# First compression layer on two halves of TensorE's output partitions in turn, and the spatial bias as one rounded product over two parts, in a two-block transformer kernel

## The chip, the cores and the metric

The kernel runs on one core of one Trainium2 chip. The metric is the device time of one execution in microseconds (us); lower is better. The time before is the median of three executions, 1076.14 us (1074.05 to 1076.87).

## What is computed

Two transformer blocks run one after the other on 256 tokens of width 1024, all in float32. Two small places of them matter here. In the first block, keys and values are compressed: blocks of 32 tokens, 16 apart, are flattened and go through two layers.

```python
def compress_blocks(src, pos, w1, w2):
    ...
    blk = src[:, idx] + pos[None, None, :, None, :]
    blk = blk.transpose(0, 1, 3, 2, 4).reshape(B, nc, NSA_KV_HEADS, CMP_BLOCK * HEAD_DIM)
    return jax.nn.silu(blk @ w1) @ w2
...
k_cmp = rms_norm(compress_blocks(kc..., cmp_pos, cmp_k_w1, cmp_k_w2), k_norm_g[0])
v_cmp = compress_blocks(vc..., cmp_pos, cmp_v_w1, cmp_v_w2)
```

In the second block, one of three branches is a spatial gate: a causal 128 by 128 mix per group of 64 features, plus a bias per group and position.

```python
def spatial_gating(u, v, ln_g, ln_b, w_s, b_s):
    v = layernorm(v, ln_g, ln_b).reshape(B, nc, CHUNK, SG_GROUPS, SG_GROUP_DIM)
    w = jnp.where(causal[None], w_s, jnp.zeros_like(w_s))
    mixed = jnp.einsum('gts,bcsgd->bctgd', w, v) + b_s.T[None, None, :, :, None]
    return u * mixed.reshape(B, S, SG_WIDTH)
```

## The kernel before

All weights come as one stream of 128x128 blocks, eight to a slot of 512 KB, in the order of their use. SyncE's queue loads slots into a ring of six (`ring`, slot_full per place); a slot is loaded again when TensorE has given it back (`give_back`, semaphore slot_used). Most products are computed to nearly float32 precision out of rounded (fp32r) parts: ScalarE rounds a slot (`round_slot`, L1321), VectorE subtracts to get the low part (`split_slot`, L1760), and TensorE's `project` adds three rounded products for each block (high by high, high by low, low by high). At most four slots are rounded ahead (`HALVES`). Two slots are taken as they come, unrounded: the first-layer weights of the compressed keys (`cmp_k_w1`) and of the values (`cmp_v_w1`). Here they are called slot A and slot B; the next ones, A+2, A+3, A+4, belong to the projections `ma0`, `ma1`, `ma2`.

ScalarE and VectorE each run one written-out program. Before an operation that reads the PSUM tile of some name, the helpers `output` and `taken` first call `ahead(name)`, which rounds (or splits) all slots up to three past the one from which that name's last product read (`slot_at[name]`). So the slot that a tile is booked on sets which roundings stand ahead of its reader in ScalarE's queue.

PSUM has eight banks; `plan_psum` gives the names of a list their banks in turn, and `claim` makes TensorE wait until the bank's previous user has been read. In the list around the change, banks 0, 1 and 2 go round: `qa0` 2, `qa1` 0, `qa2` 1, `qa3` 2, `cmp_hid_k` 0, `cmp_hid_v` 1, `ma0` 2.

The first place (L874 to L888): after `project("qa3")` and the sum of squares of `qa2`, TensorE makes `cmp_hid_k`: 16 products in plain float32, 35 rows of windows of the tokens as stationary part, 64 columns of weights moving, into partitions 0 to 34 of bank 0. Then come the sum of squares of `qa3` (`sum_squares`, a 128x128 by 128x256 float32 product that waits for ScalarE's square of `qa3`, L1337), then 16 products for `cmp_hid_v` in bank 1. A float32 product is two weight loads and two matmuls ("passes") in the trace. Then come `sb_scores(0)` and `project("ma0")`. ScalarE copies `cmp_hid_k` (L1383), makes the inverse norm of `qa3` (`inv_rms`, L1345 and L1349), and copies `cmp_hid_v`. VectorE multiplies `qa3` by it (`normalise`, L1789), which frees bank 2.

The second place (`spatial`, L1149): eight times, spread between the attention heads of the second block, a float32 product of the gate is followed by a second one that adds the bias: a 128x128 matrix of ones by `lines`, 128x256 of which only partition 0 is not zero. GpSimd has loaded `lines` (L1296 to L1301) near 309 us, in the first MLP, whose loops on ScalarE and VectorE are `for m in range(KF)` (L1567, L1544; L2095, L2108, L2023).

Of the kernel before, what the change touches and what calls it, by code (L numbers as in the profile page):

```python
# [28 lines left out]
P = 128  # L29
# [12 lines left out]
CMP_STRIDE = 16  # L42
SLOT = 8
RAW_GATES = 4
MIX_BANKS = (3, 3, 4, 4, 5, 6)
# [51 lines left out]
def stream_chunks():  # L97
# [26 lines left out]
    for name in ("cmp_k_w1", "cmp_v_w1"):  # L124
        for j in range(CMP_CHUNKS):
            out.append((name, j, None))
# [207 lines left out]
def build(nc, stream, ada, c_d, x_t, mem_t, cols_d, mats_d, buckets_d, table_d, pos_d, cmp_w2_d,  # L334
# [4 lines left out]
    with ExitStack() as ctx:  # L339
        def sb(name, shape, dt=F32):  # L340
            return ctx.enter_context(nc.sbuf_tensor(name, shape, dt))

        def sem(name):
            return ctx.enter_context(nc.semaphore(name))
# [31 lines left out]
        ada_ring = sb("ada_ring", [P, ADA_RING, D])  # L376
# [3 lines left out]
        ident_rounded = sb("ident_rounded", [P, P], F32R)  # L380
        cols = sb("cols", [P, N_COLS])
# [40 lines left out]
        lines = sb("lines", [P, 1024])  # L422
        buckets, bias_line, sg_b = lines[0:33, 0:512], lines[0:8, 512:1024], lines[0:1, :]
# [28 lines left out]
        sg_ln = ada_ring[:, 2, :].rearrange("p (w f) -> p w f", w=2)  # L452

# [48 lines left out]
        sg_ready = sem("sg_ready")  # L502
        branches_added = sem("branches_added")
# [151 lines left out]
        def _(pe):  # L655
# [218 lines left out]
            for w, n in enumerate("kv"):  # L874
                evacuated(pe, n + "c")
                if n == "v":
                    sum_squares("qa3", "halves")
                name = f"cmp_hid_{n}"
                ps = claim(name)
                for i in range(CMP_CHUNKS):  # L880
                    chunk = at["chunk"]
                    pair = take_plain()
                    for j in (2 * i, 2 * i + 1):
                        ins = mm(ps[0:CMP_ROWS, 0:HD], kc_windows[:, w, 2 * j:2 * j + 545:CMP_STRIDE],
                                 pair[:, j % 2 * HD:(j % 2 + 1) * HD], j == 0, j == 2 * CMP_CHUNKS - 1)
                    if i < CMP_CHUNKS - 1:
                        give_back(ins, chunk)
                done(ins, name)  # L888
# [260 lines left out]
            def spatial(b, c):  # L1149
                name = f"sg{b}{c}"  # L1150
                ps = claim(name)
                mm(ps[:, 0:T], sg_v[:, c, b * P:(b + 1) * P], sg_w[:, 2 * b:2 * b + 2, :], True)
                done(mm(ps[:, 0:T], mat("ones"), lines[:, b * T:(b + 1) * T], stop=True), name)

            for i in range(12):
# [23 lines left out]
                if i == 2:  # L1179
                    pe.wait_ge(sg_ln_ready, TT)  # L1180
                    pe.wait_ge(sg_w_ready, 1)
                for n in SPATIAL_AT.get(i, ()):
                    spatial(*divmod(n, TT))
# [39 lines left out]
        def _(pool):  # L1223
# [74 lines left out]
            pool.dma_start(sg_b, sg_b_d).then_inc(loaded["sg"], 16)  # L1298
            pool.wait_ge(loaded["sg"], 48)
# [11 lines left out]
        def _(act):  # L1311
# [138 lines left out]
            for w, n in enumerate("kv"):  # L1450
                copy(cmp_sb[:, w, :].rearrange("p (r c) -> p r c", r=2), f"cmp_hid_{n}",
                     bank(f"cmp_hid_{n}")[0:CMP_ROWS, 0:HD].unsqueeze(1).to_broadcast([CMP_ROWS, 2, HD]))
                if n == "k":
                    inv_rms("qa3", HD, lambda: taken("qa1"))
# [114 lines left out]
            for m in range(KF):  # L1569
# [7 lines left out]
                if m:  # L1577
                    act.wait_ge(hidden_raw, m)
                    round_hidden(m - 1)
            act.wait_ge(hidden_raw, KF)  # L1580
# [168 lines left out]
        def _(dve):  # L1749
# [349 lines left out]
            for m in range(KF):  # L2099
# [10 lines left out]
                if m:  # L2110
                    rest_of_hidden(m - 1, m - 1)
            rest_of_hidden(KF - 1, KF - 1)
# [143 lines left out]
            def sg_norm():  # L2256
                ahead("su3")
                dve.wait_ge(sg_dev_ready, 1)
                dve.wait_ge(loaded["sg"], 48)
# [184 lines left out]
```

## Time and profile before

| | |
|---|---|
| time, median of three executions | 1076.14 us (1074.05 to 1076.87) |
| profiled execution: its time, its span | 1076.19 us, 1074.4 us |
| TensorE matmuls (PE) | 1042.4 us busy, 97% of the span |
| TensorE weight loads (PEld) | 945.1 us, 88% |
| VectorE (DVE) | 813.8 us, 76% |
| ScalarE (ACT) | 617.7 us, 57% |
| GpSimd (POOL) | 48.2 us, 4% |
| chain that ended last | PE 82%, DVE 10%, issue 4%, DMA 2%, ACT 2% |
| granted clock of TensorE, mean | 0.994 |

Busy time of PE is the union of recorded matmuls, which overlap one another, so it is not a measure of how full the engine is. The chain that ended last is followed back from the last instruction, at each step to what released it. In a timeline, rows of one line, engine and operation that follow each other are merged: a start, the time from the first start to the last end, and the number of instructions.

### The profile page before, as it was taken

The page shows a single profiled execution, that of the slowest core. Times are in us where ns is not written, and L with a number is a line of the kernel's source. Part 1 is how long each engine was busy: PE and PEld are TensorE (multiplying, and loading weights), DVE is VectorE, ACT ScalarE, POOL GpSimd, SP SyncE. Part 2 cuts the span into 40 slices and gives each one's busy share as a digit, 9 for nine tenths or more (in the row PEclk, how much of TensorE's full clock was granted, in tenths as well). Part 3 has the DMA queues.
Part 4 walks back from the last instruction along what each step waited for, and adds up shares of the span by engine and source line. Part 5 has one row for each costly group of instructions (what it writes and reads, how often), then busy time and mean ns, then how long its engine had stood idle before and what let it go on. Part 6 is the DMA issues. An engine that isn't in the chain of part 4 may idle for free.

```text
span 1074.4 us, 18866 instructions
## 1 busy us (share of the span) xinstructions
PE 1042.4 (97%) x6878; PEld 945.1 (88%) x6878; DVE 813.8 (76%) x1449; ACT 617.7 (57%) x1146; POOL 48.2 (4%) x74
## 2 busy tenths in 40 slices
PE   6989989998999999999999999999999999999998
PEld 5979988997898888888888889899999998888887
DVE  6985878886998855578888777576867878888753
ACT  5486767553765544465555366697554466556531
POOL 1001100002010000000000010000000020000000
PEclk8999999999999999999999999999999999999999
DMA  9968752668686666556666665545444465666663
GB/s 359 390 235 296 228 183 80 202 224 263 232 280 191 182 191 185 188 180 193 185 188 185 188 179 159 172 138 164 131 136 139 152 179 165 191 184 189 188 189 114
DMA packets 58507, 209.46 MB, mean 195 GB/s; under 512 B 7055, under 2 KB 8463, under 8 KB 57912
## 3 DMA queue, kind: packets, MB, share of 16 engines
q1 hardware_dynamic: 52616, 185.24, 54.9%
q0 software_dynamic: 5808, 23.09, 6.2%
q8 instruction: 55, 0.90, 0.3%
q14 instruction: 28, 0.23, 0.1%
HBM read 205.14 MB, written 3.16 MB: 194 GB/s over the span
## 4 chain that ended last, share of the span: by engine, by line
PE 82%; DVE 10%; issue 4%; DMA 2%; ACT 2%; POOL 0%; DVEq 0%; ACTq 0%; POOLq 0%
PE bank L659 81%; DVE ring_rounded L1760 3%; DMA ada_ring<-in_ada 1%; ACT rounded_rounded L1321 1%; DVE body L1991 1%; PE bank L962 1%; DVE body L1960 1%; DMA ring<-in_stream 1%; DVE ada_ring L1816 0%; DVE stats L1980 0%; DMA x<-in_x_t 0%; DVE ada_ring L2079 0%; DVE stats L1977 0%; POOL turned L1270 0%; DVE body_rounded L2019 0%
## 5 line engine op out<-in xcount | busy, mean ns | idle before, releaser
L659 PE MATMUL bank<-u_rounded,rounded_rounded 128*128 128x256 f32 (+1 forms) x2136 | 544.5, 331 | 5.9 <-DVE kcat L1889 3.7
L1760 DVE TENSOR_TENSOR ring_rounded<-ring,rounded_rounded 128x1024 fp32r<-128x1024 f32 x326 | 396.5, 1224 | 116.4 <-ACT rounded_rounded L1321 109.8
L659 PE MATMUL bank<-u_rounded,ring_rounded 128*128 128x256 f32 x1504 | 424.9, 283 | 0.0
L659 PEld LDWEIGHTS bank<-u_rounded,rounded_rounded 128*128 128x128 f32 x2136 | 363.2, 190 | 49.4 <-DVE kcat L1889 4.1
L1321 ACT ACTIVATE rounded_rounded<-ring 128x1024 fp32r<-128x1024 f32 x326 | 341.8, 1054 | 106.5 <-PE bank L659 88.4
L659 PE MATMUL bank<-body_rounded,rounded_rounded 128*128 128x256 f32 (+1 forms) x1296 | 345.8, 336 | 3.7 <-DVE x L2050 1.8
L659 PEld LDWEIGHTS bank<-u_rounded,ring_rounded 128*128 128x128 f32 x1504 | 284.3, 189 | 0.1
L659 PE MATMUL bank<-body_rounded,ring_rounded 128*128 128x256 f32 x952 | 268.5, 282 | 0.0
L659 PEld LDWEIGHTS bank<-body_rounded,rounded_rounded 128*128 128x128 f32 x1296 | 222.3, 188 | 32.5 <-DVE x L2050 2.2
L659 PEld LDWEIGHTS bank<-body_rounded,ring_rounded 128*128 128x128 f32 x952 | 179.1, 188 | 0.0
L1567 ACT ACTIVATE part<-bank 128x256 f32<-128x256 f32 x65 | 25.0, 384 | 83.5 <-PE bank L659 82.3
L1816 DVE CUSTOM_DVE_ANT_0 ada_ring<-ada_ring,ada_acc,cols 128x1024 f32<-128x1024 f32 x38 | 48.1, 1278 | 9.0 <-DMA ada_ring<-in_ada 9.0
L1270 POOL TENSOR_TENSOR turned<-turned 128x256 f32<-128x256 f32 x20 | 19.3, 966 | 588.4 <-ACT turned L1590 379.2
L2095 DVE TENSOR_TENSOR part<-bank,part 128x256 f32<-128x256 f32 x65 | 27.5, 423 | 20.3 <-ACT part L1567 20.3
L1506 ACT ACTIVATE body<-body,stats 128x128 f32<-128x128 f32 (+2 forms) x64 | 25.9, 407 | 18.3 <-DVE stats L2282 15.4
L1567 ACT ACTIVATE body<-bank 128x256 f32<-128x256 f32 x44 | 16.8, 382 | 33.8 <-PE bank L659 33.8
L1544 ACT ACTIVATE body_rounded<-body 128x256 fp32r<-128x256 f32 x76 | 31.3, 412 | 8.3 <-DVE body L2173 3.9
L659 PE MATMUL bank<-rounded_rounded,u_rounded 128*128 128x512 f32 (+1 forms) x96 | 29.4, 378 | 4.4 <-DVE u_rounded L1858 4.4
L2023 DVE TENSOR_TENSOR body_rounded<-body,body_rounded 128x256 fp32r<-128x256 f32 x76 | 31.7, 417 | 1.1 <-ACT body_rounded L1544 1.0
L2095 DVE TENSOR_TENSOR body<-bank,body 128x256 f32<-128x256 f32 x44 | 18.6, 424 | 14.9 <-ACT body L1567 14.8
L659 PE MATMUL bank<-body,mats 128*128 128x256 f32 (+1 forms) x82 | 19.6, 380 | 5.6 <-ACT body L1357 5.6
L659 PEld LDWEIGHTS bank<-rounded_rounded,u_rounded 128*128 128x128 f32 x96 | 17.9, 200 | 7.5 <-issue 4.9
(270 smaller groups left out, 908.2 us busy)
## 6 DMA issues: line engine op xcount, KB each, us to landing
ring<-in_stream SPq DMA_DIRECT2D x328, 512.0 KB, 3.7
ada_ring<-in_ada POOLq DMA_DIRECT2D x32, 512.0 KB, 5.5
body<-in_ada SPq DMA_DIRECT2D x8, 512.0 KB, 9.3
ada_ring<-in_ada SPq DMA_DIRECT2D x6, 512.0 KB, 7.8
mem_parts_kept<-body_rounded POOLq DMA_DIRECT2D x2, 1024.0 KB, 6.3
body_rounded<-mem_parts_kept POOLq DMA_DIRECT2D x2, 1024.0 KB, 7.1
x<-in_x_t SPq DMA_DIRECT2D x2, 512.0 KB, 4.8
body<-in_mem_t SPq DMA_DIRECT2D x2, 512.0 KB, 6.5
```

Of the source, the lines that this page charges most:

```text
L659: return nc.tensor.matmul(out, lhs, rhs, start=start, stop=stop, skip_group_check=True)
L962: return nc.tensor.transpose(ps[:, at_col:at_col + P], src, mat("ident"))
L1270: ins = pool.tensor_tensor(row_squares[:, i, :], row_squares[:, i - 1, :], row_squares[:, i, :], ALU.add)
L1321: a(R(slot_round(q)), slot_weights(n), ACT.Copy).then_inc(slot_rounded, 1)
L1506: ins = a(dst, src, ACT.Exp, bias=stats[:, i % 2, 0, k:k + 1], accum_out=stats[:, i % 2, 1, k:k + 1])
L1544: a(R(hidden[:, i, :]), hidden_lo[:, i, :], ACT.Copy).then_inc(hidden_rounded, 1)
L1567: a(dst, bank(name)[:, T:2 * T], ACT.Copy).then_inc(half_copied, 1)
L1760: v.tensor_tensor(R(w), w, R(slot_round(q)), ALU.subtract).then_inc(slot_split, 1)
L1816: v.tensor_tensor_reduce(out=w, in0=w, in1=c_row, scale=0.5, scalar=col("ada_b", at), op0=ALU.mult, op1=ALU.add, accum_out=mod[:, at:at + ...
L1960: return v.scalar_tensor_tensor(out=out, in0=ps, scalar=HD ** -0.5, in1=b, op0=ALU.mult, op1=ALU.add)
L2023: v.tensor_tensor(R(hidden_lo[:, i, :]), hidden_lo[:, i, :], R(hidden[:, i, :]), ALU.subtract).then_inc(hidden_ready, 1)
L2095: free(v.tensor_tensor(dst, bank(name)[:, 0:T], dst, ALU.add), name)
```

## The change

The two parts are independent. In the first, the weights of keys and values are laid into the stream in turn, and TensorE makes both sums at once: `cmp_hid_k` in partitions 0 to 34 and `cmp_hid_v` in partitions 64 to 98, one product of each after the other. The sum of squares of `qa3` stands after the first four products. In the second, GpSimd loads the bias into partitions 0 and 32 of `lines`; ScalarE rounds 64 partitions of it into `sg_b_rounded` (in `ada_ring`); VectorE writes ones into `ident_rounded`, copies the rounded bias to partitions 0 to 31 of `lines`, and puts the rest (bias minus rounded bias) in partitions 32 to 63. The bias product is then one rounded product with 64 rows in place of a float32 product with 128.

```diff
+CMP_OWN = (slice(0, CMP_ROWS), slice(64, 64 + CMP_ROWS))
+SG_B_ROWS = (0, 32)
+SG_B_AT = 14
...
-    for name in ("cmp_k_w1", "cmp_v_w1"):
-        for j in range(CMP_CHUNKS):
+    for j in range(CMP_CHUNKS):
+        for name in ("cmp_k_w1", "cmp_v_w1"):
             out.append((name, j, None))
...
+        ones_rounded = ident_rounded[0:64, :]
...
+        sg_b_rounded = ada_ring[0:64, 0, :]
...
-            for w, n in enumerate("kv"):
-                evacuated(pe, n + "c")
-                if n == "v":
+            evacuated(pe, "kc")
+            evacuated(pe, "vc")
+            hid = [claim(f"cmp_hid_{n}")[CMP_OWN[w], 0:HD] for w, n in enumerate("kv")]
+            for i in range(CMP_CHUNKS):
+                chunk = at["chunk"]
+                pairs = [take_plain(), take_plain()]
+                for j in (2 * i, 2 * i + 1):
+                    for w, n in enumerate("kv"):
+                        ins = mm(hid[w], kc_windows[:, w, 2 * j:2 * j + 545:CMP_STRIDE],
+                                 pairs[w][:, j % 2 * HD:(j % 2 + 1) * HD], j == 0, j == 2 * CMP_CHUNKS - 1)
+                        if j == 2 * CMP_CHUNKS - 1:
+                            done(ins, f"cmp_hid_{n}")
+                if i < CMP_CHUNKS - 1:
+                    give_back(ins, chunk)
+                if i == 0:
                     sum_squares("qa3", "halves")
...
-                done(mm(ps[:, 0:T], mat("ones"), lines[:, b * T:(b + 1) * T], stop=True), name)
+                done(mm(ps[:, 0:T], ones_rounded, R(lines[0:64, b * T:(b + 1) * T]), stop=True), name)
...
+                    pe.wait_ge(sg_b_ready, 1)
...
-            pool.dma_start(sg_b, sg_b_d).then_inc(loaded["sg"], 16)
-            pool.wait_ge(loaded["sg"], 48)
+            for row in SG_B_ROWS:
+                pool.dma_start(lines[row:row + 1, :], sg_b_d).then_inc(loaded["sg"], 16)
+            pool.wait_ge(loaded["sg"], 64)
...
-                     bank(f"cmp_hid_{n}")[0:CMP_ROWS, 0:HD].unsqueeze(1).to_broadcast([CMP_ROWS, 2, HD]))
+                     bank(f"cmp_hid_{n}")[CMP_OWN[w], 0:HD].unsqueeze(1).to_broadcast([CMP_ROWS, 2, HD]))
...
+                if m == SG_B_AT:
+                    act.wait_ge(loaded["sg"], 64)
+                    a(R(sg_b_rounded), lines[0:64, :], ACT.Copy).then_inc(sg_b_hi_ready, 1)
...
+                if m == SG_B_AT + 1:
+                    dve.wait_ge(sg_b_hi_ready, 1)
+                    v.tensor_copy(ones_rounded, mat("ones")[0:64, :])
+                    v.tensor_copy(R(lines[0:32, :]), R(sg_b_rounded[0:32, :]))
+                    v.tensor_tensor(R(lines[32:64, :]), lines[32:64, :], R(sg_b_rounded[32:64, :]), ALU.subtract).then_inc(sg_b_ready, 1)
```

Three places of the order of instructions. On TensorE, where the compressed parts are made (`ring,turned` are the products with `cmp_k_w1` and `cmp_v_w1`, `squares,mats` the sums of squares of `qa2` and `qa3`, the `body` row is the first of `sb_scores(0)`), before:

```order
L659 MATMUL bank<-squares,mats 128x256 [waits squares_ready,bank_free3]
L659 MATMUL bank<-ring,turned 35x64 [waits bank_free0,slot_full5,bank_free3,loaded_small]
L659 MATMUL bank<-ring,turned 35x64 x15
L659 MATMUL bank<-squares,mats 128x256 [waits squares_ready,bank_free4,bank_free3]
L659 MATMUL bank<-ring,turned 35x64 [waits slot_full0,bank_free1]
L659 MATMUL bank<-ring,turned 35x64 x15
L659 MATMUL bank<-body 128x256 [waits bank_free6,bank_free4,bank_free5,bank_free1,bank_free0]
```


and now:

```order
L665 MATMUL bank<-squares,mats 128x256 [waits squares_ready,bank_free3]
L665 MATMUL bank<-ring,turned 35x64 [waits bank_free0,bank_free1,bank_free3,slot_full5,loaded_small]
L665 MATMUL bank<-ring,turned 35x64 x3
L665 MATMUL bank<-squares,mats 128x256 [waits squares_ready,bank_free4]
L665 MATMUL bank<-ring,turned 35x64 x12
L665 MATMUL bank<-ring,turned 35x64 [waits slot_full0]
L665 MATMUL bank<-ring,turned 35x64 x15
L665 MATMUL bank<-body 128x256 [waits bank_free6,bank_free4,bank_free5,bank_free1,bank_free0]
```


The sum of squares of `qa3` has moved up from after 16 of the products to after four, the two runs of 16 have become one of 28, and slot B (slot_full0) is asked for halfway through it. In both orders `ma0` comes after `sb_scores(0)` and waits for bank 2.

On ScalarE, from the rounding of slot A+3 on (`35x128` is the copy of `cmp_hid_k`; `log_ms` and `rinv` are the inverse norm of `qa3`), before:

```order
L1321 ACTIVATE rounded_rounded<-ring 128x1024 [waits slot_used,slot_full2]
L1383 ACTIVATE body<-bank 35x128 [waits bank_full0]
L1345 ACTIVATE log_ms<-bank,cols 128x256 [waits bank_full4]
L1349 ACTIVATE rinv<-log_ms 128x256 [waits bank_free0,bank_free4]
L1321 ACTIVATE rounded_rounded<-ring 128x1024 [waits slot_used,slot_full3,rinv_ready]
```


and now (L1330, L1392, L1354, L1358 are the lines L1321, L1383, L1345, L1349 of before):

```order
L1330 ACTIVATE rounded_rounded<-ring 128x1024 [waits slot_used,slot_full2]
L1330 ACTIVATE rounded_rounded<-ring 128x1024 [waits slot_used,slot_full3]
L1392 ACTIVATE body<-bank 35x128 [waits bank_full0]
L1354 ACTIVATE log_ms<-bank,cols 128x256 [waits bank_full4]
L1358 ACTIVATE rinv<-log_ms 128x256 [waits bank_free0,bank_free4]
```


The rounding of slot A+4 (slot_full3) has moved from behind the inverse norm of `qa3` to ahead of the copy of `cmp_hid_k`, since that tile is now booked on slot B and no longer on slot A. VectorE's order is unchanged here.

On VectorE, in the first MLP at m = 15 (L2035 ends the work of m = 14, L1772 splits a slot, L2107 begins the work of m = 16), the new rows stand so:

```order
L2035 TENSOR_TENSOR body_rounded<-body,body_rounded 128x256 [waits hidden_rounded]
L2126 CAST ident_rounded<-mats 64x128 [waits sg_b_hi_ready]
L2127 COPY lines_rounded<-ada_ring_rounded 32x1024
L2128 TENSOR_TENSOR lines_rounded<-lines,ada_ring_rounded 32x1024
L1772 TENSOR_TENSOR ring_rounded<-ring,rounded_rounded 128x1024 [waits slot_rounded]
L2107 TENSOR_TENSOR part<-bank,part 128x256 [waits half_copied,bank_full0]
```


Three instructions have been added ahead of a split; ScalarE has one more, a copy of 64x1024, one step of m earlier.

## Rows read from the trace of the kernel before

**Rows 1.** Chain that ended last, in order of time: start us, us, engine and line

```profile
79.13 24.06 PE bank L659 x202
...
761.85 7.21 PE bank L659 x56
```

**Rows 2.** Timeline of TensorE matmuls, 93 to 100 us: start, us, engine, line, operation, count

```profile
93.43 0.59 PE L659 MATMUL bank<-squares,mats 128*128 128x256 f32 x2
93.96 2.21 PE L659 MATMUL bank<-ring,turned 128*35 128x64 f32 x32
96.10 0.70 PE L659 MATMUL bank<-squares,mats 128*128 128x256 f32 x2
96.73 2.21 PE L659 MATMUL bank<-ring,turned 128*35 128x64 f32 x32
98.87 0.92 PE L659 MATMUL bank<-body 128*128 128x256 f32 x4
99.55 0.48 PE L659 MATMUL bank<-u_rounded,rounded_rounded 128*128 128x256 f32 x2
```

**Rows 3.** Timeline of TensorE matmuls, 113 to 115 us

```profile
113.70 0.87 PE L659 MATMUL bank<-body,pair_v 128*64 128x256 f32 x8
114.50 0.92 PE L659 MATMUL bank<-body 128*128 128x256 f32 x4
```

**Rows 4.** Timeline of ScalarE, 94 to 98 us

```profile
94.19 0.36 ACT L1337 ACTIVATE squares<-bank 128x256 f32<-128x256 f32 x1
...
95.81 1.04 ACT L1321 ACTIVATE rounded_rounded<-ring 128x1024 fp32r<-128x1024 f32 x1
96.76 0.25 ACT L1383 ACTIVATE body<-bank 35x128 f32<-35x128 f32 x1
96.91 0.46 ACT L1345 ACTIVATE log_ms<-bank,cols 128x256 f32<-128x256 f32 x1
97.40 0.42 ACT L1349 ACTIVATE rinv<-log_ms 128x256 f32<-128x256 f32 x1
```

**Rows 5.** Timeline of VectorE, 96 to 99 us

```profile
96.88 1.23 DVE L1760 TENSOR_TENSOR ring_rounded<-ring,rounded_rounded 128x1024 fp32r<-128x1024 f32 x1 [0.95 <-ACT rounded_rounded L1321]
98.03 0.48 DVE L1789 SCALAR_TENSOR_TENSOR qa<-bank,cols,rinv 128x256 f32<-128x256 f32 x1
```

**Rows 6.** DMA issues, stretches at 84.5 and 91.1 us: KB each, us to landing

```profile
ring<-in_stream SPq DMA_DIRECT2D x1, 512.0 KB, 8.7
...
ring<-in_stream SPq DMA_DIRECT2D x1, 512.0 KB, 5.6
```

**Rows 7.** Timeline of TensorE weight loads, 761 to 763 us

```profile
761.91 0.41 PEld L659 LDWEIGHTS bank<-lines,mats 128*128 128x128 f32 x2
762.34 0.41 PEld L659 LDWEIGHTS bank<-u_rounded,rounded_rounded 128*128 128x128 f32 x2
```

**Rows 8.** Timeline of TensorE matmuls, 102 to 104 us

```profile
102.12 0.40 PE L659 MATMUL bank<-u_rounded,rounded_rounded 128*128 128x256 f32 x2
102.35 0.28 PE L659 MATMUL bank<-u_rounded,ring_rounded 128*128 128x256 f32 x1
102.56 0.63 PE L659 MATMUL bank<-mats,body 35*128 35x30 f32 x4
103.20 0.59 PE L659 MATMUL bank<-mats,turned 24*128 24x24 f32 x4
```

**Rows 9.** Timelines of VectorE and ScalarE, 321 to 324 us, first MLP

```profile
321.05 0.43 DVE L2095 TENSOR_TENSOR part<-bank,part 128x256 f32<-128x256 f32 x1 [0.20 <-ACT part L1567]
...
322.24 1.23 DVE L1760 TENSOR_TENSOR ring_rounded<-ring,rounded_rounded 128x1024 fp32r<-128x1024 f32 x1
323.86 0.42 DVE L2095 TENSOR_TENSOR part<-bank,part 128x256 f32<-128x256 f32 x1 [0.40 <-ACT part L1567]
...
323.38 0.38 ACT L1567 ACTIVATE part<-bank 128x256 f32<-128x256 f32 x1 [1.17 <-PE bank L659]
```

**Rows 10.** Timeline of GpSimd, 313 us

```profile
313.49 1.09 POOL L1301 TENSOR_SCALAR_AFFINE_SELECT ada_ring<-ada_ring 128x1024 f32<-128x1024 f32 x1 [4.00 <-DMA lines<-in_sg_b]
```

More of the change, by code:

```diff
@@ L375, in build @@
         rounded = sb_split("rounded", [P, HALVES * SLOT * P])
-        ada_ring = sb("ada_ring", [P, ADA_RING, D])
+        ada_ring = sb_split("ada_ring", [P, ADA_RING, D])
         ada_acc = sb_split("ada_acc", [P, 2, D])
@@ L421, in build @@
         bias_cmp = sb("bias_cmp", [P, 8, TT, N_CMP])
-        lines = sb("lines", [P, 1024])
-        buckets, bias_line, sg_b = lines[0:33, 0:512], lines[0:8, 512:1024], lines[0:1, :]
+        lines = sb_split("lines", [P, 1024])
+        buckets, bias_line = lines[0:33, 0:512], lines[0:8, 512:1024]
         vcmp = lines[:, 0:256].rearrange("p (s c) -> p s c", s=2)
@@ L502, in build @@
         sg_ready = sem("sg_ready")
+        sg_b_hi_ready, sg_b_ready = sem("sg_b_hi_ready"), sem("sg_b_ready")
         branches_added = sem("branches_added")
@@ L871, in _ @@
             pe.wait_ge(loaded["small"], 48)
-            for w, n in enumerate("kv"):
-                evacuated(pe, n + "c")
-                if n == "v":
-                    sum_squares("qa3", "halves")
[L878 to L888, printed above, removed]
+            evacuated(pe, "kc")
[13 more added lines that the diff above has]
+                if i == 0:
+                    sum_squares("qa3", "halves")
             def cmp_turn():
@@ L2258, in sg_norm @@
                 dve.wait_ge(sg_dev_ready, 1)
-                dve.wait_ge(loaded["sg"], 48)
+                dve.wait_ge(loaded["sg"], 64)
                 for t in range(TT):
```

## Prediction

> **What bounds the kernel now.** I read the chain that ended last first, to see which engine carries the two places of the change. Both lie in long pieces of TensorE alone: one piece from 79.13 for 24.06 us over the compression, one of 7.21 us from 761.85 over the first bias product, and its like over the seven others [rows 1]. So a microsecond that TensorE saves or loses there counts in full, unless what stands next is not ready. For that I went on to the timelines of TensorE [rows 2], of ScalarE [rows 4] and of VectorE [rows 5] round the compression, since what TensorE waits for next is made there; then to the length of the slot loads [rows 6], the weight loads round a bias product [rows 7], and the nearest stretch in which TensorE goes from 128 rows to fewer [rows 8]. The first MLP, which receives the new work on VectorE and ScalarE, is in [rows 9].
>
> **Part one, TensorE alone.** Before, the first compressed layer is two bursts of 32 passes of 64 columns, 2.14 us each with the step to what follows (93.96 to 96.10, 96.73 to 98.87), that is 0.067 per pass, and between them the sum of squares of `qa3`, 0.63 (96.10 to 96.73) [rows 2]. How much two column halves gain is shown by the pair products of the attention, which also fill partitions 0 to 63 and 64 to 127 in turn: eight passes, four of 256 columns and four of 128, go by in 0.80 us (113.70 to 114.50) [rows 3]. One after the other they would take four times 0.215 (half of the 0.43 of a float32 product of 256 columns [rows 7]) and four times half of that, 1.29. So halves run side by side, less some 0.15 for going in and out. I therefore take one step of 0.067 for a pass of the keys and one of the values together.
>
> The first four products are eight passes, four steps: 93.96 to about 94.3. Then comes the sum of squares of `qa3`, which needs ScalarE's square of it, done at 94.19 + 0.36 = 94.55 [rows 4]. TensorE waits some 0.3, does it in 0.63, and is at 95.25. The other 28 products are 28 steps of 0.067, 1.88: `sb_scores(0)` begins at 97.13 in place of 98.87. It lasts 0.68 to the start of `ma0`'s first matmul (98.87 to 99.55 [rows 2]), so TensorE is ready for `ma0` at 97.8, 1.7 us earlier than before.
>
> **Part one, what is late next.** `ma0` writes bank 2, whose last user is `qa3`, and that bank is free only when VectorE has multiplied `qa3` by its inverse norm. Before, this was done at 98.03 + 0.48 = 98.51 [rows 5], a microsecond ahead of need. Now one more rounding, of slot A+4, stands on ScalarE ahead of the copy of `cmp_hid_k` and of that inverse norm. The rounding of A+3 begins at 95.81 and the next instruction at 96.76, 0.95 later [rows 4]; ScalarE has no gap there. So A+4 goes from 96.76 to 97.71, the copy (0.15 to the next) to 97.86, the logarithm (0.49) to 98.35, the inverse norm (0.42) ends at 98.77 [rows 4]. VectorE is free since 98.11 [rows 5]; its 0.48 ends at about 99.28, and TensorE starts `ma0` at about 99.33. Its first weight load, which before ran under the matmuls ahead of it, is now in the open: squares with a load in the open take 0.70 and without it 0.59 [rows 2], so 0.11. That is 99.44 against 99.55: **part one brings 0.1 us**, and the remaining 1.6 becomes a wait of TensorE for bank 2. Everything that ScalarE and VectorE do next is at most 0.8 later (`qa3` at 98.8 in place of 98.03), while TensorE meets their first result only after `ma0` and its followers, over 4 us later; I cost that at nothing. The cover has one condition: slot A+4 must have landed at 96.76. It was issued at 91.04 and took 5.6 [rows 6], so 96.6. If it comes later, copy, norm, bank and `ma0` come later by as much.
>
> **Part two, TensorE.** A bias product now costs 0.43 us (weight load at 761.91, the next product's at 762.34) [rows 7]. A rounded pass of 256 columns costs half of 0.23 (102.12 to 102.35, two passes), 0.12 [rows 8]. If that were all, eight products would bring 8 x (0.43 - 0.12) = 2.5 us. But the new product has 64 rows and its neighbours 128. The trace has one place of that sort: after a rounded pass at 102.35 the product with 35 rows begins at 102.56, 0.21 later and not 0.12 [rows 8], so 0.09 is lost, and the weights aren't loaded ahead. Coming back from 35 columns costs the same sort of thing: the squares at 96.10 take 0.11 longer than those at 93.43, their load in the open [rows 2]. So I take for one bias product: 0.10 to stop, 0.11 to load, 0.11 for the columns, 0.10 to stop again, 0.11 for the next load in the open, together 0.53 against 0.43. Eight of them lose 0.8; as the columns and loads are rounded up, I put 0.7. Bounds: -2.5 if 64 rows need no stop; and on the other side the step from 35 to 24 rows, where four passes with loads of 0.11 take 0.64 (102.56 to 103.20) [rows 8], 0.20 over 0.44: with 0.20 per stop a product costs 0.73, and eight lose 2.4. I take the middle value since it comes from the step between 128 rows and fewer. **Part two costs 0.7 us.**
>
> The Trainium skill, TensorEngine Tiling (Array Packing), Key Properties, says that a change of the tiling mode drains TensorE, though not a change of tile within it; it has no price. By it the gain of 2.5 would not come either, and the column halves within the run of 28 would stay free of it.
>
> **Part two, the preparation.** VectorE gets three instructions: two of 1024 columns, which I cost as the split of 1024, 1.23, and a small one, 0.3: 2.8 us. ScalarE gets about 1.05. In the first MLP VectorE works 2.4 of 2.81 us per step (321.05 to 323.86, idle 0.40) and ScalarE waits 1.17 per step [rows 9]. The split at 322.24 ends at 323.47, when TensorE has just ended the next output (ScalarE takes it at 323.38); the slot is three outputs on, so two outputs, 5.6 us, lie between: 2.8 fits. VectorE catches up within eight steps of the 17 left. The DMA of the bias is in by 313.49 [rows 10], some 10 us ahead of ScalarE's new wait; a second small one adds half a microsecond. All of this costs nothing.
>
> **Sum.** 1076.19 (the profiled execution, 0.05 above the median) - 0.1 + 0.7 = **1076.8 us**.
>
> **Rivals.**
> (a) No stop at 64 rows: part two brings 2.5. For it: both products read and write whole banks, and only rows change. Against it: the 0.09 and the load in the open at 35 rows. 1076.19 - 0.1 - 2.5 = 1073.6.
> (b) Bank 2 is not the wait and part one keeps its 1.7, for instance as A+4's rounding overlaps what follows. Against it: ScalarE's timeline is full. With part two at +0.7, 1075.2; with (a) as well, 1072.0, the only way to more than 0.3% of gain.
> (c) The two halves don't run side by side at 64 columns: 64 passes as before, `sb_scores(0)` at 98.87, `ma0` as before; 1076.9. Against it: rows 3. The Trainium skill, TensorE: Matmul & The Clock Gate, says under The mechanism that a weight load overlaps running matmuls only where the row group differs, which column halves do not offer; the loads of 0.41 that lie under matmuls at 761.91 disagree with it for the plain case.
> (d) Slower: slot A+4 lands late, and ScalarE stands at its rounding with the copy, the norm and bank 2 behind it. It decides from the first microsecond past 96.76. The slot issued at 84.5 took 8.7 [rows 6]; with that, A+4 lands at 99.7, `ma0` begins 2.9 later, at 102.3, 2.8 later than before: 1076.19 + 2.8 + 0.7 = 1079.7.
>
> **Chances.** What a measurement can tell from no change is 0.3%, 3.2 us: faster is below 1072.9, slower above 1079.4. The forecast gets 0.50, (a) 0.22, (b) 0.08 (of which 0.04 with (a)), (c) 0.12, (d) 0.08. Of (a) some part lies below 1072.9, as the three executions before differ by 2.8 us among themselves; with the rest of (b) that is 0.10 for faster. Most of (d) is slower: 0.07. The range goes from just below (a), 1073.2, to 1078.8, which takes in the dearer stops of part two (1078.5) and leaves out most of (d) and the best case of (b).
>
> **What would show it.** TensorE's timeline: passes of `ring,turned` in a run of 56 that takes about 1.9 us; then a new idle time of about 1.5 before `ma0` that ends with VectorE's `qa`; no such wait before. ScalarE: two roundings in a row ahead of the copy of 35 rows. Bias products: a weight load of 64 rows that begins only when the matmul before it has ended, and 0.5 to the load after next; if the load stands under the matmul and the product takes 0.12, (a) is right. Wrong altogether: `ma0` starting at 97.8, or a new wait of TensorE in the first MLP.

## The result and the profile after

| | before | after |
|---|---|---|
| median, times measured beside each other | 1076.15 us (1074.02 to 1076.93, six) | 1080.33 us (1079.11 to 1082.52, six) |
| ratio | | 1.0046 [1.0033, 1.0059] |
| profiled execution: its time, its span | 1076.19 us, 1074.4 us | 1082.52 us, 1080.8 us |
| TensorE's mean granted clock in it | 0.994 | 0.991 |

The change is slower by 0.46% (the ratio gives 5.0 us, the two medians lie 4.2 apart). The forecast was 1076.8, with a range up to 1078.8. The profiled execution of after is the slowest of its six, so sizes come from stages, and totals from the ratios. The helpers have moved a few lines: `mm` is L665, a rounding L1330, a split L1772, the logarithm and inverse norm L1354 and L1358, the multiplication of `qa` by its norm L1801.

**The first place.** TensorE's timeline of after (start, us, count, and in brackets the idle time before and who ended it) answers to [rows 2]:

```profile
93.54 0.59 PE L665 MATMUL bank<-squares,mats 128*128 128x256 f32 x2
...
98.12 0.65 PE L665 MATMUL bank<-ring,turned 128*35 128x64 f32 x8 [3.98 <-DVE qa L1801]
98.70 1.22 PE L665 MATMUL bank<-squares,mats 128*128 128x256 f32 x2
99.85 3.21 PE L665 MATMUL bank<-ring,turned 128*35 128x64 f32 x56
102.99 1.04 PE L665 MATMUL bank<-body 128*128 128x256 f32 x4
...
104.74 0.51 PE L665 MATMUL bank<-u_rounded,rounded_rounded 128*128 128x256 f32 x2 [0.71 <-DVE qa L1801]
```

TensorE stands idle for 3.98 us ahead of its first product, which in before began right behind the squares. Then all it does takes nearly twice as long: the squares 1.15 to the next (98.70 to 99.85) against 0.63. The granted clock of TensorE says why. It is the third number from the end in these rows, the windows of after; ahead of it stand the busy times of PE, PEld, DVE, ACT and POOL, behind it the DMA share and GB/s:

```profile
94.00:98.00 4.00, 0.13 (x1) 0.00 (x0) 1.73 (x2) 2.89 (x7) 1.60 (x2) 0.81 0.47 190
98.00:103.00 5.00, 4.88 (x67) 3.93 (x67) 1.23 (x1) 1.62 (x2) 0.00 (x0) 0.50 0.40 113
...
104.00:105.00 1.00, 0.29 (x3) 0.26 (x3) 0.80 (x2) 0.93 (x3) 0.00 (x0) 1.00 0.69 258
```

0.50 is the lower of its two levels, 1.2 GHz. TensorE was granted 1.00 before it stood idle (92 to 94 us), the clock fell while it waited, and it stayed at 0.50 for all of the compressed layer. The profile shows this order in time; that the wait brings the fall is shown by the kernel with the claim alone, below. The chain of waits of after, in order of time, names what the first product waited for:

```profile
84.59 10.39 DMA ring<-in_stream
95.04 1.06 ACT rounded_rounded L1330
96.13 1.34 DVE ring_rounded L1772
97.47 0.41 DVE qa L1801
```

The last of these is VectorE's multiplication of `qa2`, which frees bank 1. In the trace of before the same instruction stands here, in a row that the prediction did not read (VectorE):

```profile
95.45 0.48 DVE L1789 SCALAR_TENSOR_TENSOR qa<-bank,cols,rinv 128x256 f32<-128x256 f32 x1
```

It ends at 95.93. That was in time for the second burst, at 96.73 [rows 2], which alone wrote bank 1. After the change both banks are claimed ahead of the first product, which stood at 93.96. Behind the wait comes the one that was predicted. ScalarE's inverse norm and VectorE's multiplication of `qa3` in after answer to [rows 4, 5]:

```profile
103.75 0.42 ACT L1358 ACTIVATE rinv<-log_ms 128x256 f32<-128x256 f32 x1
104.20 0.48 DVE L1801 SCALAR_TENSOR_TENSOR qa<-bank,cols,rinv 128x256 f32<-128x256 f32 x1 [4.27 <-ACT rinv L1358]
```

**The stage in one number.** From the start of the last squares pass ahead of it (the second of two that a row of `squares,mats` merges: 93.65 before, 93.75 after) to the first weight load of `ma0` (99.52 and 104.74) it is 5.87 us before and 10.99 after: 5.1 more. Of this 4.05 is the later first product, 1.07 the stretch behind it. Another 0.3 is lost between `ma0` and 116 us: there the matmuls of after lie 5.4 further behind those of before than at 88 us.

**The second place.** TensorE's weight loads at the first bias product of after (against [rows 7]):

```profile
768.00 0.18 PEld L665 LDWEIGHTS bank<-lines_rounded,ident_rounded 64*128 64x128 f32 x1 [0.33 <-issue]
768.31 0.30 PEld L665 LDWEIGHTS bank<-u_rounded,rounded_rounded 128*128 128x128 f32 x2
```

and the matmuls at the same place:

```profile
767.47 0.60 PE L665 MATMUL bank<-ada_ring,vcat 128*128 128x256 f32 x2
768.00 0.38 PE L665 MATMUL bank<-lines_rounded,ident_rounded 64*128 64x256 f32 x1
```

The load of 64 rows isn't ahead of its matmul: it begins at 768.00, and the next product's at 768.31. In the chain the stage runs from 767.63 to 848.59 (80.96 us), where before it ran from 761.85 [rows 1] to 842.29 (80.44):

```profile
767.63 7.30 PE bank L665 x55
...
848.59 1.56 PE bank L665 x13
```

and the end of the stage in the chain of before:

```profile
842.29 1.55 PE bank L659 x13
```

Eight products cost 0.5 us more. That is clear of the scatter: the stage takes 80.4 to 80.6 in the six traces with the bias product of before, and 80.9 to 81.0 in the four with 64 rows.

**The preparation in the first MLP.** VectorE in after, the copy and the subtraction:

```profile
334.13 0.67 DVE L2127 CAST lines_rounded<-ada_ring_rounded 32x1024 fp32r<-32x1024 f32 x1
334.82 1.22 DVE L2128 TENSOR_TENSOR lines_rounded<-lines,ada_ring_rounded 32x1024 fp32r<-32x1024 f32 x1
```

The copy of 1024 columns took 0.67, not 1.23. The splits fall some 2.5 us behind and are back in step five splits later; TensorE has no idle time there, and its matmuls stay as far behind those of before (5.7 us) at 300, 345 and 600 us.

### The profile page after: what moved, and what is told of

The parts are those of the page before. It is cut to its first block, busy times and chain, and to the rows that moved or that the text cites. A ratio compares the mean times of both kernels' runs of the same rounds, so it can differ in the third digit from the quotient of the medians.

```text
span 1080.8 us, 18857 instructions
## 1 busy us (share of the span) xinstructions
PE 1043.6 (97%) x6870; PEld 943.7 (87%) x6870; DVE 815.7 (75%) x1452; ACT 617.8 (57%) x1147; POOL 49.6 (5%) x75
## 4 chain that ended last, share of the span: by engine, by line
PE 81%; DVE 10%; issue 4%; DMA 3%; ACT 2%; POOL 0%; DVEq 0%; ACTq 0%; POOLq 0%; SPq 0%
PE bank L665 80%; DVE ring_rounded L1772 3%; DMA ring<-in_stream 2%; ACT rounded_rounded L1330 1%; DMA ada_ring<-in_ada 1%; DVE body L2003 1%; DVE body L1972 1%; PE bank L969 1%; DVE ada_ring L1828 1%; DVE stats L1992 0%; DMA x<-in_x_t 0%; DVE ada_ring L2091 0%; DVE stats L1989 0%; POOL turned L1278 0%; DVE body_rounded L2031 0%
## 5 line engine op out<-in xcount | busy, mean ns | idle before, releaser
L665 PE MATMUL bank<-u_rounded,rounded_rounded 128*128 128x256 f32 (+1 forms) x2136 | 544.8, 332 | 6.5 <-DVE kcat L1901 3.7
L1772 DVE TENSOR_TENSOR ring_rounded<-ring,rounded_rounded 128x1024 fp32r<-128x1024 f32 x326 | 396.8, 1225 | 122.3 <-ACT rounded_rounded L1330 115.8
L665 PE MATMUL bank<-u_rounded,ring_rounded 128*128 128x256 f32 x1504 | 425.7, 284 | 0.0
L665 PEld LDWEIGHTS bank<-u_rounded,rounded_rounded 128*128 128x128 f32 x2136 | 363.3, 190 | 50.6 <-DVE kcat L1901 4.1
L1330 ACT ACTIVATE rounded_rounded<-ring 128x1024 fp32r<-128x1024 f32 x326 | 341.9, 1054 | 109.4 <-PE bank L665 86.9
L665 PE MATMUL bank<-body_rounded,rounded_rounded 128*128 128x256 f32 (+1 forms) x1296 | 346.2, 336 | 3.6 <-DVE x L2062 1.8
L665 PEld LDWEIGHTS bank<-u_rounded,ring_rounded 128*128 128x128 f32 x1504 | 285.2, 190 | 0.1
L665 PE MATMUL bank<-body_rounded,ring_rounded 128*128 128x256 f32 x952 | 269.2, 283 | 0.0
L665 PEld LDWEIGHTS bank<-body_rounded,rounded_rounded 128*128 128x128 f32 x1296 | 222.7, 188 | 32.3 <-DVE x L2062 2.3
L665 PEld LDWEIGHTS bank<-body_rounded,ring_rounded 128*128 128x128 f32 x952 | 179.5, 189 | 0.0
L2107 DVE TENSOR_TENSOR part<-bank,part 128x256 f32<-128x256 f32 x65 | 27.5, 423 | 18.0 <-ACT part L1576 17.9
L1515 ACT ACTIVATE body<-body,stats 128x128 f32<-128x128 f32 (+2 forms) x64 | 25.9, 407 | 18.3 <-DVE stats L2299 15.3
L665 PE MATMUL bank<-rounded_rounded,u_rounded 128*128 128x512 f32 (+1 forms) x96 | 29.4, 379 | 4.6 <-DVE u_rounded L1870 4.6
L2035 DVE TENSOR_TENSOR body_rounded<-body,body_rounded 128x256 fp32r<-128x256 f32 x76 | 31.8, 418 | 1.1 <-ACT body_rounded L1553 1.0
L2107 DVE TENSOR_TENSOR body<-bank,body 128x256 f32<-128x256 f32 x44 | 18.7, 424 | 15.2 <-ACT body L1576 15.1
L665 PE MATMUL bank<-body,mats 128*128 128x256 f32 (+1 forms) x82 | 19.4, 379 | 5.6 <-ACT body L1366 5.6
L665 PEld LDWEIGHTS bank<-rounded_rounded,u_rounded 128*128 128x128 f32 x96 | 18.0, 200 | 7.8 <-issue 5.2
```

Source lines behind the costliest of these rows:

```text
L665: return nc.tensor.matmul(out, lhs, rhs, start=start, stop=stop, skip_group_check=True)
L1330: a(R(slot_round(q)), slot_weights(n), ACT.Copy).then_inc(slot_rounded, 1)
L1515: ins = a(dst, src, ACT.Exp, bias=stats[:, i % 2, 0, k:k + 1], accum_out=stats[:, i % 2, 1, k:k + 1])
L1772: v.tensor_tensor(R(w), w, R(slot_round(q)), ALU.subtract).then_inc(slot_split, 1)
L2035: v.tensor_tensor(R(hidden_lo[:, i, :]), hidden_lo[:, i, :], R(hidden[:, i, :]), ALU.subtract).then_inc(hidden_ready, 1)
L2107: free(v.tensor_tensor(dst, bank(name)[:, 0:T], dst, ALU.add), name)
```

## The experiments

In what follows "the stage" is the same distance, last squares pass to first load of `ma0`: 5.87 in before. All ratios are to the kernel before, run on the same chip in turn.

**Each part by itself.** The first kernel has the diff of the compressed layer alone, the second that of the bias alone.

> The change's first part alone (compression in two halves), with the bias product as before. Theory W (the loss is the early wait for bank 1): TensorE stands still ahead of the first product of the keys until VectorE has read qa2, 3 to 4 us, at half clock after it; time 1079.7, that is 3.6 over the 1076.15 of before, and 0.6 under the 1080.33 of the full change. Rival P (the loss is in the bias part, in its products or its preparation): about 1076 to 1077.

> The change's second part alone (rounded bias product with 64 rows), with the compression as before. Theory W: eight products, each 0.08 us dearer since TensorE stops on both sides of it, 0.6 in all: 1076.8, no new wait in the first MLP. Rival P: 1079 to 1080.

Measured: part one 1.0041 [1.0022, 1.0059], stage 10.42; part two 1.0002 [0.9988, 1.0015], stage 5.96, and the spatial stage 0.5 us longer. So the loss is part one's. Part two's 0.5 is seen in the spatial stage and is below what a ratio can tell.

**The bank of the values out of the way.** The full change, with `cmp_hid_v` in bank 7, which is free here, and the turn of the other banks kept:

```diff
-    out += ["cmp_hid_k", "cmp_hid_v", "ma0", ...]
+    out += ["cmp_hid_k", None, "ma0", ...]
-    out = [f"sbo{b}" for b in range(4)] + ...
+    out = ["cmp_hid_v"] + [f"sbo{b}" for b in range(4)] + ...
```

and the same with `cmp_hid_k` booked one slot earlier, so that ScalarE and VectorE keep their order of before (`slot_at["cmp_hid_k"] -= 1`).

> The full change, but cmp_hid_v lies in bank 7 (free since about 66 us) in place of bank 1; the banks of all other names stay. Theory W: no wait ahead of the first product, TensorE goes on at about 93.96 at full clock, 28 steps of a pair of passes at 0.062 take 1.8 us, then ma0 waits for bank 2 until about 99.3; time 1076.7 (before, -0.1 for the first part, +0.6 for the bias). Rival D (a slot that lands later than before causes the loss, whatever the bank): 1079 to 1080, with a wait of ScalarE for the ring's DMA that passes on to ma0.

> As the one before, and cmp_hid_k is booked on slot A again, so that ScalarE rounds slot A+4 after the inverse norm of qa3, as before the change. Theory W with a second wait for bank 2 behind the first: copy of cmp_hid_k at 97.2, norm done at 98.3, ma0 at about 98.9 in place of 99.3: 0.5 less than the kernel before this one, 1076.2. Rival (the booking doesn't matter, since ScalarE waits for something else there): same time within 0.2.

Measured: 1.0006 [0.9993, 1.0019], stage 6.55; and 1.0002 [0.9989, 1.0016], stage 6.46. TensorE of the first of the two:

```profile
92.19 0.48 PE L667 MATMUL bank<-ring,turned 128*35 128x64 f32 x8
93.79 0.67 PE L667 MATMUL bank<-squares,mats 128*128 128x256 f32 x2 [1.12 <-ACT squares L1348]
94.39 2.01 PE L667 MATMUL bank<-ring,turned 128*35 128x64 f32 x56
96.33 0.92 PE L667 MATMUL bank<-body 128*128 128x256 f32 x4
...
98.44 0.51 PE L667 MATMUL bank<-u_rounded,rounded_rounded 128*128 128x256 f32 x2 [1.19 <-DVE qa L1803]
```

The products start at once and the clock stays at 1.00, and with that nearly the whole loss is gone. The row of 56 passes shows what the halves are worth: 1.94 us (94.39 to 96.33), 28 steps of 0.069, so a pass of the keys and one of the values go side by side at the price of one. All 32 steps would take 2.2, where before took twice 2.14 [rows 2]. The 2.1 that this saves becomes two waits: 1.12 for ScalarE's square of `qa3`, and 1.19 for bank 2 (counted from start to start they cost 1.3 and 1.5). Booking the tile one slot earlier changed the stage by 0.1, where 0.5 was expected. The wait for bank 2 fell to 0.82, but that for the square rose to 1.34, as slot A+2 landed 0.2 later; with one trace of each, the order on ScalarE is small here, and its size is not shown.

**The claim alone.** Nothing of the change: in the kernel before, one line claims bank 1 ahead of the first product, all else as it was.

```diff
+            claim("cmp_hid_v")
             for w, n in enumerate("kv"):
```

> The kernel before the change with one line more: TensorE claims bank 1 (cmp_hid_v's) ahead of the first product of the keys. No halves, no other order, bias as before. Theory W (the early wait for the reader of qa2 is the loss): TensorE stands for 2 to 4 us ahead of the products of the keys; if that makes the granted clock fall to 0.5 the two runs of 32 passes take 3.4 each in place of 2.1; time between 1078 and 1081. Rival (the loss needs the two halves or the new order): 1075 to 1076.

Measured: 1.0056 [1.0036, 1.0076], stage 9.98. TensorE's timeline:

```profile
96.69 3.43 PE L659 MATMUL bank<-ring,turned 128*35 128x64 f32 x32 [2.82 <-issue]
100.05 0.70 PE L659 MATMUL bank<-squares,mats 128*128 128x256 f32 x2
100.68 2.22 PE L659 MATMUL bank<-ring,turned 128*35 128x64 f32 x32
```

VectorE's multiplication of `qa2`:

```profile
96.12 0.48 DVE L1790 SCALAR_TENSOR_TENSOR qa<-bank,cols,rinv 128x256 f32<-128x256 f32 x1
```

The windows, with the granted clock as above:

```profile
93.00:96.00 3.00, 0.87 (x6) 0.47 (x4) 1.03 (x1) 2.08 (x4) 1.17 (x2) 1.00 0.63 257
96.00:100.00 4.00, 3.31 (x32) 3.32 (x32) 1.82 (x3) 1.48 (x4) 0.45 (x1) 0.57 0.32 95
```

One wait that is moved ahead makes a loss as large as that of the change, without any of its products. The profile names no releaser for this wait (`issue`); the only line that was added asks for bank 1, and the multiplication that frees it ends at 96.60, the first product begins at 96.69. The run shows the two prices apart: 2.9 us more of waiting (3.20 from the last squares pass to the first product, where it is 0.31 in before), and then 32 passes in 3.36 us (96.69 to 100.05) at the lower clock, which take 2.15 (100.68 to 102.83) at the upper: 1.2 more. As the wait is all that was added, it brought the fall of the clock as well, which neither trace of before has here.

**Before, a second time.**

> The kernel before a second time, for its trace. The landing of slot A+2 differed between executions from 0.5 ahead of the last squares pass ahead of the compression to 1.2 behind it. If before is insensitive to it, its distance from that pass to the first matmul of `ma0` is again 5.9 to 6.1 with whatever landing; if the landing carries part of the loss, it is over 6.5 where the landing is late. Idle time of TensorE ahead of the first product stays under 0.2.

Its stage is 5.87 again, to the hundredth, though slot A+2 landed later. ScalarE's rounding of that slot (in brackets its idle time, for the DMA) begins at 92.80, 0.20 behind the last squares pass (92.60, the second of the row of TensorE from 92.38), where in the first trace of before it began at 93.22, 0.43 ahead of it (93.65):

```profile
92.80 1.06 ACT L1321 ACTIVATE rounded_rounded<-ring 128x1024 fp32r<-128x1024 f32 x1 [2.14 <-DMA ring<-in_stream]
```

and TensorE of the same trace:

```profile
92.38 0.60 PE L659 MATMUL bank<-squares,mats 128*128 128x256 f32 x2
92.90 2.22 PE L659 MATMUL bank<-ring,turned 128*35 128x64 f32 x32
```

This landing isn't late enough to tell whether the order of before is insensitive to it. Two other traces with that order, of the kernels with the bias over 128 rows (below), settle it: there the rounding begins 0.58 and 0.70 behind the pass, and the second burst waits for the same multiplication of `qa2`. In the first of these two:

```profile
96.46 2.22 PE L664 MATMUL bank<-ring,turned 128*35 128x64 f32 x32 [0.37 <-DVE qa L1799]
```

Their stages are 6.32 and 6.34. So before can stand a rounding up to some 0.3 us behind the pass, and pays for what comes later (part two alone, with 0.39, has 5.96). That allows a fair comparison. The second burst of before is due 3.08 behind the pass. With the multiplication's end as after had it (4.11 behind the pass), before's stage would be 1.1 longer, 7.0; with that of part one alone (3.54) 6.4; with that of the claim alone (3.10) 6.0. These are estimates. Measured were 10.99, 10.42 and 9.98: 4.0 more in each of the three. So 1.1 of after's 5.1 is the landing of that one execution. In the claim alone the 4.0 is the wait and the lower clock behind it. In the other two the wait, less the landing, is about as long, and what the halves save is lost again to the lower clock and to bank 2; that this comes out at the same 4.0 is chance.

**The rest of part one's gain.** In part one alone, `cmp_hid_v` is in bank 7, the names behind it move up one (so `ma0` is in bank 1, free early), the squares of `qa3` come after 16 products, and the booking is that of before. The second has the mended bias (below) too.

```diff
-    out += ["cmp_hid_k", "cmp_hid_v", "ma0", ...]
+    out += ["cmp_hid_k", "ma0", ...]
-                if i == 0:
+                if i == 3:
                     sum_squares("qa3", "halves")
```

> The first part alone, mended: cmp_hid_v in bank 7, and the names behind it move up one bank, so that ma0 takes bank 1 (qa2's) and no longer bank 2 (qa3's); the sum of squares of qa3 after 16 products and not after four; cmp_hid_k booked on slot A. Theory W: no wait for bank 1 or 2, pairs of passes at 0.063, ma0 starts 1.5 to 1.9 us earlier against the squares of qa2 than before; what is late next is VectorE's first softplus, which leaves 1.2: 1.2 under the kernel before, ratio 0.999. Rival (halves don't pay at all once the waits are gone): ratio 1.000, ma0 not earlier.

> The mended first part with a mended bias: the rounded product keeps 128 rows (partitions 0 to 31 the rounded part, 32 to 63 the rest, the others zero), so TensorE has no stop at it. Theory W: 1.2 from the first part and 8 x 0.31 = 2.5 from the bias, 3.7 under the kernel before, ratio 0.9966. Rival (the stop is not due to the 64 rows): the bias brings nothing or costs 0.6, ratio 0.999.

Measured: 1.0019 [1.0010, 1.0029] and 0.9997 [0.9985, 1.0009]. The stage is 4.41 and 4.62: the gain of 1.5 is there, and lost again 5 us on. TensorE of the first:

```profile
101.48 0.59 PE L660 MATMUL bank<-mats,turned 24*128 24x24 f32 x4 [1.40 <-ACT body L1387]
102.00 1.65 PE L660 MATMUL bank<-body 128*128 128x256 f32 x4
103.44 1.92 PE L660 MATMUL bank<-body,mats 128*128 128x256 f32 x6
```

and ScalarE's copy of `ma0`:

```profile
100.97 0.36 ACT L1387 ACTIVATE body<-bank 128x256 f32<-128x256 f32 x1
```

The gates' turn (24 rows) now shares bank 1 with `ma0` and waits 1.40 for ScalarE's copy of it, and then the clock falls to 0.50 once more (from 102 to 105 us): the step from 102.00 to 103.44 is 1.44, where the same two pieces of before stand 0.75 apart:

```profile
103.72 0.92 PE L659 MATMUL bank<-body 128*128 128x256 f32 x4
104.47 1.04 PE L659 MATMUL bank<-body,mats 128*128 128x256 f32 x6
```

So I took that bank away too: `ga_turn` in bank 7.

```diff
-    out += ["ga_turn", "ma1", ...]
+    out += [None, "ma1", ...]
-    out = ["cmp_hid_v"] + [f"sbo{b}" for b in range(4)] + ...
+    out = ["cmp_hid_v", "ga_turn"] + [f"sbo{b}" for b in range(4)] + ...
```

> The version of part one alone with `cmp_hid_v` in bank 7, `ma0` in bank 1 and the squares of `qa3` after 16 products, and now also the gates' turn (`ga_turn`, 24x24) in bank 7, so that it no longer waits for ScalarE's copy of `ma0`. In the version without this it waited 1.40 for that copy and began at 101.48, and TensorE's clock was halved afterwards. Theory 1 (the bank of `ma0` held the gain back): `ga_turn` about 1.4 earlier, near 100.1, no idle time over 0.3 there, no half clock behind it, time about 1.4 to 3 us below that version, ratio to before 0.998 to 0.9995. Theory 2 (VectorE was the last wait anyway): the next TensorE product (128x256 from `body`) reads what VectorE ends at 102.03 + 0.28 = 102.3, so the idle time only moves, to about 1.6 us ending at 102.3; half clock as before, ratio 1.001 to 1.003. I hold theory 2 for the likelier, since VectorE's row of 102.03 stands behind a split of 1.22 that is not touched.

> The same with the spatial bias rounded over all 128 rows. Both theories give the time of the version above less 2.5 us (the spatial stage without a stop): ratio 0.9955 to 0.997 under theory 1, 0.999 to 1.001 under theory 2. If it comes below 0.996 it is the fastest version.

Measured: 1.0011 [1.0000, 1.0023] and 0.9986 [0.9976, 0.9996]. TensorE of the first:

```profile
99.83 0.62 PE L662 MATMUL bank<-mats,turned 24*128 24x24 f32 x4
100.38 0.92 PE L662 MATMUL bank<-body 128*128 128x256 f32 x4
102.17 1.15 PE L662 MATMUL bank<-body,mats 128*128 128x256 f32 x6 [0.87 <-DVE body L1919]
...
103.78 0.51 PE L662 MATMUL bank<-u_rounded,rounded_rounded 128*128 128x256 f32 x2 [0.34 <-DVE cmp_turned L1930]
```

and VectorE, the piece that TensorE waits for at 102.17:

```profile
101.84 0.28 DVE L1919 TENSOR_TENSOR body<-body,mats 128x128 f32<-128x128 f32 x1
```

The gates' turn is at once behind the products with 35 rows now, and the wait has moved on, to 0.87 for VectorE and 0.34 for VectorE again. The expected theory 2 is right on the place, has the wait too long (1.6), and is wrong on the clock, which stays at 1.00 in this trace. In that of its sister with the mended bias, where the same piece waits less, it falls to 0.50 (102 to 105 us), and six passes that span 1.15 here take 1.92:

```profile
101.52 1.92 PE L667 MATMUL bank<-body,mats 128*128 128x256 f32 x6 [0.56 <-DVE body L1929]
```

Measured over a longer stretch, to the thirty-first projection pass behind this place, the distance from the last squares pass is 17.7 in both traces of before and 18.3 in this one: every microsecond that TensorE saved has become idle time, and a little more.

**The bias with 128 rows.** The kernel before with part two alone, but with the rounded ones over all 128 partitions, and the parts of `lines` that hold zeros rounded by one more copy:

```diff
-        ones_rounded = ident_rounded[0:64, :]
+        ones_rounded = ident_rounded[:, :]
-                    v.tensor_copy(ones_rounded, mat("ones")[0:64, :])
+                    v.tensor_copy(ones_rounded, mat("ones"))
+                    v.tensor_copy(R(lines[64:P, :]), lines[64:P, :])
-                done(mm(ps[:, 0:T], ones_rounded, R(lines[0:64, ...]), stop=True), name)
+                done(mm(ps[:, 0:T], ones_rounded, R(lines[:, ...]), stop=True), name)
```

> The kernel before with the bias as one rounded product of 128 rows alone. Theory (stop due to 64 rows): weight loads of the bias product lie under the matmul ahead, 0.12 each in place of 0.43, 2.5 us less, ratio 0.9977. Rival (rounded after float32 makes the stop whatever the rows): as with 64 rows, ratio 1.0005.

> The kernel before with only the spatial bias as one rounded product of 128 rows, a second time. It was 0.9959 [0.9944, 0.9975], 3.9 us, of which its spatial stage shows 2.4. If the whole is the stage: ratio 0.9978 +- 0.001. If something else brings the rest: 0.996 again.

Measured: 0.9959 [0.9944, 0.9975] with a median of 1071.62, and the second time 0.9969 [0.9956, 0.9982], 1072.42. **This version is faster than both kernels.** The loads at its bias product, in the second of the two:

```profile
763.68 0.19 PEld L664 LDWEIGHTS bank<-lines_rounded,ident_rounded 128*128 128x128 f32 x1
763.89 0.19 PEld L664 LDWEIGHTS bank<-u_rounded,rounded_rounded 128*128 128x128 f32 x1
```

the gate product ahead of it:

```profile
763.46 0.60 PE L664 MATMUL bank<-ada_ring,vcat 128*128 128x256 f32 x2
```

and the start and the end of the stage in the chain:

```profile
763.62 6.90 PE bank L664 x55
...
841.61 1.56 PE bank L664 x13
```

The load at 763.68 lies under the product that began at 763.46, and the next load comes 0.21 later, not 0.31. The stage takes 77.99 us (763.62 to 841.61), 2.45 less than before. Two more pairs of kernels differ by this bias: part one mended (1.0019 and 0.9997) and the gates in bank 7 (1.0011 and 0.9986). They differ by 2.4 and 2.7 us, as the stage does. The ratios here say 4.4 and 3.3 us; 2.45 lies within the interval of the second (1.9 to 4.7) and just outside that of the first (2.7 to 6.0). Nowhere else behind 300 us does either trace gain on that of before, so the rest has no place in what was changed, and it stays open.

## Why the prediction was wrong

- **The step that failed** is the first of "Part one, TensorE alone": "The first four products are eight passes, four steps: 93.96 to about 94.3." It lets the first product start where it did before. The order of instructions said otherwise: the row of that product had `bank_free1` added to its waits, and the prediction asked of bank 2 alone when it comes free; the wait for bank 1 it put at nothing. The answer stood in before's trace: bank 1 is free at 95.93, so the first product begins at 96.0, two microseconds late. In after it began 4.05 late. The claim alone, with none of the new products, made 1.0056, and with `cmp_hid_v` in bank 7 the loss was gone (1.0006).
- **The size of it.** These two microseconds became 4.05 in after, since slot A+2 took 10.39 us to land and ScalarE's rounding of it, the inverse norm of `qa2` and VectorE's split all stood behind it. Rival (d) had this mechanism for slot A+4; here it was two slots earlier, and it is the new wait that made most of it: the order of before would have lost 1.1 by the same landing, by the estimate above. In after's ScalarE no rounding of A+3 or A+4 waited for a DMA.
- **The clock** was not in the prediction. The trace of before shows what a wait of this length can bring, not far ahead of the place. TensorE stands idle for 3.71 us ahead of 79.13, and the clock is at 0.50 for the two microseconds after 80:

```profile
79.13 0.50 PE L659 MATMUL bank<-u_rounded,rounded_rounded 128*128 128x256 f32 x2 [3.71 <-DVE kcat L1889]
```

  The windows of before at the same place:

```profile
78.00:80.00 2.00, 0.87 (x6) 0.87 (x7) 1.95 (x7) 2.00 (x8) 0.00 (x0) 0.90 0.00 0
80.00:82.00 2.00, 2.00 (x11) 2.00 (x11) 2.00 (x7) 1.34 (x3) 0.55 (x1) 0.50 0.67 127
```

  In after, behind the wait, it cost 2.0 (the first eight passes 0.58 for 0.28, squares 1.15 for 0.63, 56 passes 3.14 for 1.94), as much as the halves saved (2.1). From `sb_scores(0)` to `ma0`, with the wait for bank 2, it took 1.75 for 0.65, and that is the 1.07 by which the stretch from the first product to `ma0` came out longer than before.
- **Column halves side by side**: right. 0.067 for a step of two passes was predicted, 0.069 measured (where the clock is full). So rival (c) is out.
- **Bank 2 next**: right, with 1.19 of idle time in the kernel where nothing else waits, and 0.71 in after; 1.5 was predicted. Rival (b) is out. The wait for the square of `qa3` was put at 0.3 and came to 1.1, as A+2 was rounded 0.9 later against the last squares pass in that execution than in the profiled one of before. (Behind that wait the prediction comes to 95.25, where 94.55 + 0.63 is 95.18: a slip of 0.07 that changes nothing.)
- **A stop at 64 rows**: right in kind. 0.53 against 0.43 was predicted for a product, eight times 0.1, put at 0.7; 0.5 was measured. Rival (a), 2.5 us of gain, is what 128 rows give, and 64 rows do not. The Trainium skill, TensorEngine Tiling (Array Packing), Key Properties, has a drain where the tiling mode changes: the two kernels with the one and the other number of rows agree with it (80.96 and 77.99 us for the stage).
- **The first MLP costs nothing**: right, with the copy half as dear as put (0.67, not 1.23).
- **The sum** with measured terms in place of the predicted ones: 5.4 up to 116 us and 0.5 for the bias give 1076.19 + 5.4 + 0.5 = 1082.1. Two spells at the lower clock elsewhere, with what lies near them, add 0.3 (last section); the profiled execution has 1082.52.

## What to carry over

When a claim, or any wait, is moved ahead in an engine's queue, look up for each resource in it who frees it last and when, and compare that with the new time of need, also where it never waited before. An idle time of TensorE of some three microseconds was paid for twice here, by itself and by the clock behind it. When two traces are compared, look first at whether the transfers ahead of the place landed at the same point of each: 1.1 of the 5.1 us here was that. And when a product has fewer rows than its neighbours, price the stop on both sides first; filling the rows with zeros was worth 2.9 us against the version with 64 rows, for one more copy.

## What the runs showed that I had not expected

- The granted clock fell to 0.50 in waits of 3.98 us (after) and 2.82 us (the claim alone), and for the products behind a wait of 1.40 us too (`ga_turn` in bank 1). It did not fall with idle times of 0.72, 0.87 and 0.34 within 10 us (the gates in bank 7), nor with 1.12 and 1.19 (the values in bank 7), but it did with a single one of 0.56 (the gates in bank 7, with the mended bias). So the length of a wait doesn't settle it, and what does is not shown here. A 64-column float32 pass takes 0.067 us at the upper level and 0.105 at the lower.
- A float32 pass of 64 columns on partitions 0 to 34 and one on 64 to 98 in turn cost 0.069 together.
- The landing of one and the same slot of 512 KB came from 0.5 us ahead of the last squares pass to 1.2 behind it, between executions of nearly the same program. A new wait of TensorE turns such spread into time.
- Spells at the lower clock come at about 80 us in every trace, at 151 in the first of before but neither in the second nor in after, and in some traces (after, and the two of the bias with 128 rows among them) between 260 and 290 us. No part of the change stands there, and why they come isn't settled. Against before, after gains 0.9 us where it lacks the spell at 151, loses 1.5 at its own at 288 and wins back 0.3 in waits at 267: the 0.3 in the sum above.
